# A seven-product stage in the last down projection as well, with the weight blocks' sums moved from VectorE to GpSimd

## What is computed

```python
for l in range(2):
    h = rmsnorm(x, norm1_g[l])
    ...                                     # projections, three mixers, w_out
    x = x + mixed @ w_out[l]                # 2048 x 2048
    h2 = rmsnorm(x, norm2_g[l])
    x = x + square(relu(h2 @ w_up[l])) @ w_down[l]   # 2048 -> 8192 -> 2048
```

## Time and profile before

| | |
|---|---|
| median of 3 runs | 2040.28 us (2040.23 to 2040.54) |
| time of the profiled execution | 2040.27 us |
| its span, first to last instruction | 2038.5 us |
| busy in the span | PE 2032.6, DVE 1519.6, ACT 1088.2, POOL 213.1 us |
| TensorE's granted clock | 1.00 |

### The profile page before, as it was taken

How to read it: one execution, slowest core, us unless ns; L and a number is a source line. 1 busy time by engine, 2 the same in 40 slices (tenths; PEclk the granted TensorE clock), 3 DMA queues, 4 the chain that set the end, 5 groups by cost and what they waited for, 6 DMA issues and landing times.

```text
span 2038.5 us, 27071 instructions
## 1 busy us (share of the span) xinstructions
PE 2032.6 (100%) x10626; PEld 1707.2 (84%) x10626; DVE 1519.6 (75%) x1967; ACT 1088.2 (53%) x1412; POOL 213.1 (10%) x220
## 2 busy tenths in 40 slices
PE   9999999999999999999999999999999999999999
PEld 8887788888888888888888877888888888888887
DVE  7767566789779769867677775667997797798674
ACT  6557644455456446544445586444554564564442
POOL 6253100000000000001023531000000000000000
PEclk9999999999999999999999999999999999999999
DMA  9477866677668667766665679666776686677663
GB/s 304 132 229 187 224 199 179 184 220 226 188 198 243 196 199 212 223 191 188 185 176 145 215 200 227 186 183 189 218 225 192 197 247 189 196 223 214 185 194 124
DMA packets 186334, 409.24 MB, mean 201 GB/s; under 512 B 14058, under 2 KB 22736, under 8 KB 186208
## 3 DMA queue, kind: packets, MB, share of 16 engines
q1 hardware_dynamic: 178064, 379.52, 60.7%
q0 software_dynamic: 7968, 27.91, 7.6%
q10 hardware_dynamic: 176, 0.09, 0.0%
HBM read 377.95 MB, written 2.12 MB: 186 GB/s over the span
## 4 chain that ended last, share of the span: by engine, by line
PE 99%; DMA 0%; issue 0%; SPq 0%; DVE 0%
PE psum L599 24%; PE psum L623 23%; PE psum L626 12%; PE psum L603 12%; PE psum L668 9%; PE psum L671 4%; PE psum L633 2%; PE psum L637 2%; PE psum L634 2%; PE psum L719 1%; PE psum L718 1%; PE psum L722 1%; PE psum L733 1%; PE psum L805 1%; PE psum L784 0%; PE psum L830 0%
## 5 line engine op out<-in xcount | busy, mean ns | idle before, releaser
L927 ACT CAST w_hi<-raw_ring 128x1024 fp32r<-128x1024 f32 (+1 forms) x720 | 745.6, 1043 | 794.1 <-PE psum L626 360.1
L1137 DVE TENSOR_TENSOR w_lo<-raw_ring,w_hi 128x1024 fp32r<-128x1024 f32 (+1 forms) x668 | 815.8, 1229 | 380.5 <-ACT w_hi L927 378.3
L623 PE MATMUL psum<-xt,w_hi 128*128 128x512 f32 x2048 | 513.3, 392 | 0.3 <-issue 0.3
L623 PEld LDWEIGHTS psum<-xt,w_hi 128*128 128x128 f32 x2048 | 368.8, 189 | 67.0 <-issue 0.7
L626 PEld LDWEIGHTS psum<-xt,w_lo 128*128 128x128 f32 x2048 | 279.4, 190 | 20.0
L626 PE MATMUL psum<-xt,w_lo 128*128 128x256 f32 x2048 | 285.5, 282 | 0.0
L599 PE MATMUL psum<-w_hi,xt 128*128 128x512 f32 (+1 forms) x1152 | 281.5, 386 | 0.0
L599 PEld LDWEIGHTS psum<-w_hi,xt 128*128 128x128 f32 x1152 | 202.4, 188 | 40.8 <-issue 2.9
L599 PE MATMUL psum<-w_hi,ht_hi 128*128 128x512 f32 x512 | 203.0, 397 | 0.0
L599 PE MATMUL psum<-w_hi,ht_lo 128*128 128x512 f32 x512 | 199.8, 390 | 0.0
L668 PE MATMUL psum<-w_hi,ht_lo 128*128 128x512 f32 x384 | 149.5, 389 | 0.0
(11 more groups left out here) (210 smaller groups left out, 2279.0 us busy)
## 6 DMA issues: line engine op xcount, KB each, us to landing
raw_ring<-in_w_up_dram SPq DMA_DIRECT2D x256, 512.0 KB, 4.1
raw_ring<-in_w_down_dram SPq DMA_DIRECT2D x256, 512.0 KB, 4.4
raw_ring<-in_w_in_dram SPq DMA_DIRECT2D x128, 512.0 KB, 4.7
raw_ring<-in_w_out_dram SPq DMA_DIRECT2D x64, 512.0 KB, 5.0
w_lo<-raw_ring POOLq DMA_DIRECT2D x28, 512.0 KB, 7.0
lo_own<-raw_ring POOLq DMA_DIRECT2D x24, 512.0 KB, 6.9
raw_ring<-in_w_in_dram SPq DMA_DIRECT2D x16, 256.0 KB, 2.8
x<-in_x_dram SPq DMA_DIRECT2D x8, 256.0 KB, 7.5
```

The costliest lines, as they stand in the source:

```text
L623: pe.matmul(bank[:, f, :], w_hi[:, w, j, f * P:(f + 1) * P], both, start=kt == 0, stop=False, skip_group_check=True)
L927: act.copy(w_hi[:, u % AHEAD, :, 0:cols], raw_ring[:, u % RAWS, :, 0:cols]).then_inc(hi_ready, 1)
L1137: dve.tensor_tensor(w_lo[:, u % AHEAD, :, 0:cols], raw_ring[:, u % RAWS, :, 0:cols], w_hi[:, u % AHEAD, :, 0:cols].bitcast(F32), ALU.subtr ...
```

## The change

The last quarter's down projection does its half d = 0 as a pair stage with seven products too (16 units, from `DOWN3` on). Only the half d = 1 is left in plain units: 16 units from `TAIL` on, two chunks (c = 2, 3) of eight units. `totals` is complete at step `TAIL`, and `add_totals` does two additions in each of the next four steps and then signals `x_summed`, for which the next layer's first transposes and the output's stores wait.

The four weight sums of every seven-product pair move from VectorE's `split_lo` and `first_sums` to a new GpSimd function `weight_sums`. GpSimd's list holds them seven units ahead of the pair, merged with the accumulating DMAs, which stand six units ahead. `split_lo` now waits for `t2_ready` or `t_raw_ready`, and GpSimd's first sum waits for `t_lo_ready` of the pair before. GpSimd's tables for the second layer wait for `s_done` in place of `relu2`.

```diff
-CHUNKS = NPROJ + 4 + 4 + 4 * LOOPS + 8
+CHUNKS = NPROJ + 4 + 4 + 4 * LOOPS + 2
...
-SEVENS = LOOPS * 2 * len(SEVEN)
+SEVENS = (LOOPS * 2 + 1) * len(SEVEN)
+TAIL = DOWN3 + 2 * KPS
+TURNS = LOOPS + 1
+SUMMED_PAIR += [DOWN3, DOWN3 + 8]
 NEGATED_AHEAD = 6
+SUMS_AHEAD = 7
+SEVEN_UNITS = [LOOP0 + LOOP_UNITS * i + 16 * d + 2 * kp for i in range(LOOPS + 1) for d in range(2 if i < LOOPS else 1) for kp in SEVEN]
...
-for _c in range(2):
-    for _n in range(2):
-        T_USE[DOWN3 + 16 + 4 * _c + 3 + 2 + 2 * _n] = ("x1", 2 * _c + _n)
-T_USE[DOWN3 + 16 + 8 + 3 + 2] = ("x1", 4)
+for _n in range(4):
+    T_USE[DOWN3 + 21 + 2 * _n] = ("x1", _n)
+T_USE[DOWN3 + 29] = ("x1", 4)
...
-            for st in mlp_steps(DOWN3, ["down"]):
+            for st in mlp_steps(LOOP0, ["first"]):
+                do_mlp(Place(l, LOOPS), *st)
+            for st in mlp_steps(TAIL, ["down"]):
                 do_mlp(pl, *st)
...
+                    if use[0] == "x1" and c < 2:
+                        pe.wait_ge(x_summed, pl.l + 1)
...
+                    if k == 0 and c == 2:
+                        pe.wait_ge(pair_out, pl.l * LAYER_OUTS + LOOPS * TURN_OUTS + 2)
+                    if k == 0 and c == 3:
+                        pe.wait_ge(totals_out, (pl.l + 1) * TURNS)
+                    rows_unit(pl, s, ht, (2 * k, 2 * k + 1), n, k == 0, k == UPC - 1, CW)
...
             def split_lo(pl, u, cols=CW, then=None):
-                after = seven_at(pl, u + 1)
-                if after is not None and after[0] == 0:
-                    first_sums(pl, u + 1)
...
+                seven = seven_at(pl, u)
+                dve.wait_ge(hi_ready, pl.unit(u + 1))
+                if seven is not None:
+                    dve.wait_ge(t_raw_ready if seven[0] else t2_ready, seven[1] + 1)
+                dve.tensor_tensor(w_lo[:, u % AHEAD, :, 0:cols], raw_ring[:, u % RAWS, :, 0:cols],
+                                  w_hi[:, u % AHEAD, :, 0:cols].bitcast(F32), ALU.subtract).then_inc(split_done, 1)
                 if then is not None:
                     then()
...
+                if s == TAIL:
+                    dve.wait_ge(sevens_done, (pl.l + 1) * SEVENS)
+                    dve.tensor_tensor(totals[:, :, :], psum[:, 0:4, :], totals[:, :, :], ALU.add).then_inc(totals_out, 1)
+                if TAIL < s < TAIL + 5:
+                    for n_sum in range(2):
+                        add_totals(pl, 2 * (s - TAIL - 1) + n_sum)
...
+            def weight_sums(pl, u):
+                number = seven_at(pl, u)[1]
+                for v in (u, u + 1):
+                    pool.wait_ge(raw_loaded[v % RAWS], pl.at(16 * UNITS // RAWS, 16 * (v // RAWS + 1)))
...
+                if number:
+                    pool.wait_ge(t_lo_ready, number)
+                pool.tensor_tensor(t_raw[:, 0, :], b22, b12, ALU.subtract)
+                pool.tensor_tensor(b12, b12, b11, ALU.subtract).then_inc(t1_ready, 1)
+                pool.wait_ge(t1_ready, number + 1)
+                pool.tensor_tensor(t_raw[:, 1, :], b22, b12, ALU.subtract).then_inc(t2_ready, 1)
+                pool.wait_ge(t2_ready, number + 1)
+                pool.tensor_tensor(t_raw[:, 2, :], b21, t_raw[:, 1, :], ALU.subtract).then_inc(t_raw_ready, 1)
...
-                for n, u in enumerate(SUMMED_UNITS):
+                for _, u in sorted([(v - NEGATED_AHEAD, v) for v in SUMMED_UNITS] + [(v - SUMS_AHEAD, v) for v in SEVEN_UNITS]):
+                    if u in SEVEN_UNITS:
+                        weight_sums(pl, u)
+                        continue
```

More of the change, by code:

```diff
@@ L141 @@
 EXPS_X1, EXPS_X2 = 0, {OUT_LAST[c] + 1: c for c in range(4)}
-EXPS_X1_LATE = {DOWN3 + 16 + 4 * c + 4: c for c in range(3)}
+EXPS_X1_LATE = {DOWN3 + 22 + 2 * c: c for c in range(3)}
 G1, G1_NEXT, G2, A_GAIN, SUBLN, NLAM, SINK, NSINK, ONE, PARS = 0, 16, 32, 48, 49, 50, 51, 67, 83, 84
@@ L320, in encoder @@
         totals_out = sem("totals_out")
+        x_summed = sem("x_summed")
         t1_ready, t_raw_ready, t_hi_ready, t_lo_ready = (sem(f"{n}_ready") for n in ("t1", "t_raw", "t_hi", "t_lo"))
@@ L364, in mlp_steps @@
         def mlp_steps(first, kinds):
-            s, n = first, {UP0: 13, LOOP0: 17, DOWN3: 17 + 4 * LOOPS}[first]
+            s, n = first, {UP0: 13, LOOP0: 17, TAIL: 17 + 4 * LOOPS}[first]
             for kind in kinds:
-                if kind == "pair":
-                    for d in range(2):
+                if kind in ("pair", "first"):
+                    for d in range(2 if kind == "pair" else 1):
                         for m in range(2 * KPS):
@@ L380, in mlp_steps @@
                 else:
-                    for c in range(8):
-                        for k in range(4):
-                            yield s, "down", c // 4, c, k, n
+                    for c in (2, 3):
+                        for k in range(UPC):
+                            yield s, "down", None, c, k, n
                             s += 1
@@ L427, in pair_at @@
             w = u - LOOP0 + LOOP_UNITS * (pl.i or 0)
-            if 0 <= w < LOOPS * LOOP_UNITS and w % LOOP_UNITS < PAIR_UNITS:
+            if 0 <= w < TAIL - LOOP0 and w % LOOP_UNITS < PAIR_UNITS:
                 return w // LOOP_UNITS, w % PAIR_UNITS // (2 * KPS), w % (2 * KPS)
@@ L448, in sums_made @@
         def sums_made(pl, s, part, c, k, lag):
-            if part == "up" and c == 2 and k == lag and (s < LOOP0 or pl.i < LOOPS - 1):
-                return 0, pl.l * 2 * LOOPS + 2 * (0 if s < LOOP0 else pl.i + 1)
+            if part == "up" and c == 2 and k == lag:
+                return 0, pl.l * 2 * TURNS + 2 * (0 if s < LOOP0 else pl.i + 1)
             if part == "pair" and c == 0 and k == lag:
-                return 1, pl.l * 2 * LOOPS + 2 * pl.i + 1
+                return 1, pl.l * 2 * TURNS + 2 * pl.i + 1
             return None
@@ L525, in load_down @@
             def load_down(pl, u, c, k):
-                row = (c // 4 + 2 * LOOPS) * (D_FF // 8) + k * 2 * P
-                load(pl, u, w_down, D, pl.l * (D_FF * D) + (row * D + (c % 4) * CW), CW)
+                row = LOOPS * D + k * 2 * P
+                load(pl, u, w_down, D, pl.l * (D_FF * D) + row * D + c * CW, CW)
             def load_pair(pl, u, turn, d, m):
@@ L540, in mlp @@
                     load_pair(pl, u, *pair_at(pl, u))
+                elif part == "pair" and pl.i == LOOPS:
+                    load_down(pl, u, 2, u - LOOP0 - 2 * KPS)
                 elif part == "pair":
@@ L544, in mlp @@
                     n = c * UPC + k + FIRST_LOADS
+                    load_up(pl, u, n // UPC, n % UPC)
+                else:
+                    n = c * UPC + k + FIRST_LOADS
                     if n < 4 * UPC:
[L546 to L552, removed]
+                        load_down(pl, u, n // UPC, n % UPC)
                     elif pl.l < DEPTH - 1:
@@ L570, in _ @@
                     break
-                sp.wait_ge(evicted[n % 2], Place(DEPTH - 1).evictions(n) + 1)
+                if c < 2:
+                    sp.wait_ge(x_summed, DEPTH)
+                else:
+                    sp.wait_ge(evicted[n % 2], Place(DEPTH - 1).evictions(n) + 1)
                 sp.dma_start(out[0, :, c * CW:(c + 1) * CW].rearrange("(r p) n -> p r n", p=P),
@@ L755, in use_t @@
                     n = NPROJ + c if use[0] == "x2" else CHUNKS - 4 + c
-                    if use[0] == "x1" and c >= 2 and s < PU:
+                    if use[0] == "x1" and c < 2:
+                        pe.wait_ge(x_summed, pl.l + 1)
+                    elif use[0] == "x1" and c >= 2 and s < PU:
                         pe.wait_ge(evicted[n % 2], pl.at(EVICTIONS[n % 2], 1))
@@ L1095, in mlp @@
                     m = CHUNKS - 4 + cc
-                    square_x(pl, 0, cc, pl.at(16, 16 + 2 * cc), [(evicted[m % 2], pl.evictions(m) + 1)])
+                    square_x(pl, 0, cc, pl.at(16, 16 + 2 * cc), [(x_summed, pl.l + 1) if cc < 2 else (evicted[m % 2], pl.evictions(m) + 1)])
             def tables():
@@ L1147, in split_lo @@
                     dve.tensor_tensor(t_lo[:, :, :], t_raw[:, :, :], t_hi[:, :, :].bitcast(F32), ALU.subtract).then_inc(t_lo_ready, 1)
[L1149 to L1158, removed]
             def token_sums(b):
@@ L1210, in add_totals @@
                 if n == 0:
[L1211 to L1215, removed]
+                    dve.wait_ge(pair_out, (pl.l + 1) * LAYER_OUTS)
+                    dve.wait_ge(totals_out, (pl.l + 1) * TURNS)
+                last = add_sums(totals, 0, n)
+                link(last) if n < 7 else last.then_inc(x_summed, 1)
             def add_second(pl, n):
                 if n == 0:
-                    dve.wait_ge(pair_out, pl.at(LOOPS * TURN_OUTS, 8, TURN_OUTS))
+                    dve.wait_ge(pair_out, pl.at(LAYER_OUTS, 8, TURN_OUTS))
                     dve.wait_ge(sevens_done, sevens_after(pl, 1))
@@ L1505, in mlp @@
                     add_second(pl, k)
-                if DOWN3 + 4 <= s < DOWN3 + 12:
-                    add_totals(pl, s - DOWN3 - 4)
```

(4 more changed lines are left out.)

33 lines of the change are left out of this document (11 added, 22 removed).

## The result

The changed kernel takes 2107.36 us (median of four runs, 2105.83 to 2108.85) against 2040.41 beside it (four runs, 2040.23 to 2040.96): 1.0326 times as long, 95% interval 1.0314 to 1.0338. It is slower by 67 us; forecast were 2100, between 2055 and 2118. The execution profiled took 2105.83 us, the earlier one 2040.27, so 65.56 us are to be found.

A forecast was written before the change was run, and what follows sets the result against it. The matmul count on TensorE was taken to set the time while VectorE's splits come in time. 2040.27 + 56 (six pair stages) + 2.6 (half stages) + 1.3 (`x_summed`) = 2100 us, range 2055 to 2118.

The forecast's parts named there:

- The mechanism: VectorE and GpSimd instructions each reading two SBUF operands run one after the other; a sum holds VectorE up to 1.15 us.
- an operand in PSUM is exempt: Instructions with an operand in PSUM, such as quarters, totals and evictions, run beside GpSimd's SBUF reads without collision.
- whoever comes first: Of two colliding two-operand SBUF instructions on VectorE and GpSimd, the one that comes first goes first.
- The walk: Pair stage, period by period between `t_lo` ends: together 82.9 us, last `t_lo` at 850.3 for 838.24; chance 0.50 for 2076 to 2110.
- The stage's end: After a pair stage's last `t_lo`, seven matmuls are left, 1.6 us; the stage ends 6.8 us later than before.
- The quarter: Fourth quarter of d = 1 comes 4.8 us after the last `t_lo`; TensorE stops about 2.5 us at the next up unit.
- The half stage: New seven-product half d = 0 of the last quarter's down projection: +1.3 us against 43.54 for plain units, twice, +2.6.
- the tail's first bank: After the new half stage, the wait for the tail's first bank costs some 0.8 us more.
- The wait for `x_summed`: End of layer 0: `x_summed` comes at 14.9 us after unit `TAIL`, TensorE asks at 13.6, costing +1.3 us.
- The slack: Second pair of d = 0 needs `t_lo` at 783.14 and gets it at 782.25, a slack of 0.9 us.
- Rival 2: Reads collide, but sums fall mostly under PSUM work and waits: 2040 to 2075 us, 2068 the likeliest; chance 0.25.
- Rival 3: VectorE wins the ties and accumulating DMAs come late, queued behind waiting sums: 2110 to 2125 us; chance 0.15.

The follow-up runs named there:

- write-only run: Changed kernel with each weight sum replaced by a GpSimd write of all of `t_raw` that reads nothing, sums left out: 2037.66 us (one run).
- the stage alone: Changed kernel with the four weight sums back on VectorE, nothing of them on GpSimd: 2037.43 us against 2040.51, ratio 0.9984.
- the sums alone: Kernel before the change with only the weight sums of its six pair stages moved to GpSimd: 2099.38 us, ratio 1.0287.
- run with idle subtractions: Kernel before, VectorE's sums kept, plus eight GpSimd subtractions of 128 x 128 constants in each pair, results never read: 2106.51 us (one run).

## Why the prediction was right

**The mechanism** was read correctly from the earlier trace rows: two instructions that each read two operands from SBUF take turns. The write-only run shows that it is the reads, and the runs with the stage alone and with the sums alone that the sums are the whole loss. Two parts of the rule were weaker than they were put. That an operand in PSUM is exempt was read from a copy, which has one operand; the changed kernel's quarters show it for two. And whoever comes first doesn't always go first: in the run with idle subtractions the one that comes at 805.61, under `s_lo`, is out only at 809.92, when five of VectorE's instructions back to back have gone ahead of it; in the changed kernel a sum that comes under `s_lo` (803.65) goes right behind it. What decides this isn't shown.

**The walk.** Forecast were periods of 15.9, 11.1, 11.1, 12.4, 11.1, 10.2 and 11.1 us; measured 16.02, 11.15, 11.14, 12.41, 11.14, 10.16 and 11.14, the sum within 0.3 us. The price of 1.15 us for a sum behind a split held: the sum from 805.71 ends at 807.98, 1.15 us after the split above it (804.52 and 2.31). That split in turn took 1.09 us more than the 1.22 of one alone.

**The stage's end** was mis-sized: 1.6 us from the last `t_lo` to the end, measured 2.85. The step counted the seven matmuls behind `t_lo`. The last pair takes its second unit first, and TensorE stood at that unit's split, out at 868.93, with 19 matmuls (4.5 us, from 868.98 to 873.44) to go. So `t_lo`, out at 870.59, was never what it waited for. **The quarter** was mis-sized the other way: 2.5 us forecast, 1.3 measured, since the later end of the stage covers the rest. The two terms share one end point, VectorE's row (the fourth quarter is out 4.7 us after `t_lo`, 4.8 forecast), so the two errors cancel for a reason. Their sum was 9.3 forecast and 9.8 measured: six stages 58.7 instead of 56.

**The half stage** costs +2.15 twice, not +1.3: the same mis-sized end, less the 0.8 us for the tail's first bank, a wait that isn't among TensorE's. **The wait for `x_summed`** is 1.9, not 1.3. With the sums on VectorE it is 1.3; that the other 0.6 come from VectorE's entering the tail later is argued from the chain alone. These terms, 2.3 us, with 2.7 from the stages, 0.5 ahead of the first pair stage and 0.1 unplaced, are the 5.6 us between the forecast 2100.2 and 2105.8.

**What the profile was to show**: splits of 2 us and more, sums of 1.3 to 2.3, `t_lo` 11 us apart, stages of 90 to 93 us and the half at 43 to 46 came as said. Wrong was the place of the wait: TensorE waits 39.9 us for `w_lo` (36 times), not for `t_lo`. The up stages didn't stay at 89 us either, since the wait for the quarter lies in them (90.7). The slack was read at the wrong operand too: the split of the pair's second unit is needed before `t_lo`. It didn't enter the sum, as the walk goes to the end of the stage.

**The rivals.** Rival 2 (holes take it up) is seen in one place, the first pair of d = 0, and is worth next to nothing at the second pair (0.1 of 1.17 us). Rival 3's late DMAs did not come; its range, 2110 to 2125, lies above the result.

## What to carry to other kernels

An instruction moved from VectorE to GpSimd doesn't leave VectorE if it reads SBUF while VectorE runs instructions with two operands in SBUF: here four sums gave VectorE back 2.4 us in each pair, and its period from `t_lo` to `t_lo` still grew from 8.75 to 11.15. So look for holes in VectorE's row first (the first pair was free there), or move work that only writes. And measure slack at the first operand that the waiting engine needs, which here was a split, ten matmuls ahead of the `t_lo` that looked tight.

## What the runs showed of the hardware

GpSimd's writes of 128 x 1536 in 1.39 us leave VectorE's two-operand splits at 1241 ns, the figure of the kernel before. An operand in PSUM takes an instruction out of the collision: 24 quarters beside sums took 0.68 us, as the 32 others. Short reads are no remedy: with 128 x 128 subtractions VectorE's instructions took 0.26 us more once the two engines took turns, one subtraction between two instructions, and a subtraction took 1058 ns on average. The first one behind each stage's second `t_lo` took 4.31 us. And GpSimd's arithmetic delays the DMAs issued behind it: 27.0 us of TensorE's time in 12 waits of the run with idle subtractions.
